# Gate and up products of the second token group by seven block products in place of eight

## What is computed

```
def _swiglu(x, w_gate, w_up, w_down):
    return (jax.nn.silu(x @ w_gate) * (x @ w_up)) @ w_down
...
x = _layer_norm(ALPHA * x + 0.5 * _swiglu(x, p['ffn1_gate'], p['ffn1_up'], p['ffn1_down']), p['ln1_g'], p['ln1_b'])
... projection, short convolution and sparse attention ("mix"), then attention into 256 memory tokens
x = _layer_norm(ALPHA * x + 0.5 * _swiglu(x, p['ffn2_gate'], p['ffn2_up'], p['ffn2_down']), p['ln4_g'], p['ln4_b'])
```

## Time and profile before

| | |
|---|---|
| time, median of 3 runs | 2527.73 us (2526.59 to 2529.33) |
| span of the profiled execution, first to last instruction | 2523.5 us |
| TensorE matmuls busy | 2437.7 us, 97% of the span, 16311 matmuls |
| VectorE, ScalarE, GpSimd busy | 36%, 39%, 55% |
| DMA | 245 MB, 97 GB/s in the mean, the 16 engines 33% busy |
| share of TensorE in the chain that ended last | 85% |

### The profile page before, as it was taken

The page is one execution under the profiler, slowest core; times in us unless marked ns, Lnnn a source line. Parts: engine busy times, 40 slices in busy tenths (PEclk is TensorE's granted clock), DMA queues, the critical chain, the costliest instruction groups (busy, mean ns, idle before and its releaser), DMA issues.

```text
span 2523.5 us, 39960 instructions
## 1 busy us (share of the span) xinstructions
PE 2437.7 (97%) x16311; PEld 2217.3 (88%) x16311; DVE 920.9 (36%) x1775; ACT 982.3 (39%) x1736; POOL 1376.1 (55%) x860
## 2 busy tenths in 40 slices
PE   8999999999999999998999999999899999999998
PEld 8888889888999999987789877888659899999998
DVE  1000002266810004277452689997264333000003
ACT  4333333534333233455543533333473435333231
POOL 4776665534666666422252676766405246666663
PEclk9999999999999999999999999999999999999999
DMA  4444532453233222533121234333402122433322
GB/s 145 123 119 117 159 94 75 139 156 104 83 94 91 86 84 79 141 107 125 45 76 35 70 102 106 110 92 100 166 1 88 48 68 81 121 109 101 92 84 69
DMA packets 425661, 245.00 MB, mean 97 GB/s; under 512 B 23008, under 2 KB 415328, under 8 KB 424720
## 3 DMA queue, kind: packets, MB, share of 16 engines
q1 hardware_dynamic: 389712, 197.88, 27.4%
q10 hardware_dynamic: 33200, 32.56, 4.0%
q0 software_dynamic: 2576, 12.07, 1.3%
HBM read 218.79 MB, written 21.74 MB: 95 GB/s over the span
## 4 chain that ended last, share of the span: by engine, by line
PE 85%; ACT 4%; DVE 4%; POOL 3%; issue 2%; DMA 1%; ACTq 0%; DVEq 0%; POOLq 0%
PE LIN L768 77%; PE TR L1109 1%; POOL WL L2093 1%; PE LIN L845 1%; PE TR L821 1%; ACT WH L1159 1%; POOL XL L2133 1%; ACT PR L1608 1%; ACT PT L1633 1%; PE LIN L1057 1%; PE TR L922 1%; DVE SC L1714 1%; PE TR L1096 1%; DVE PR L2032 1%; DVE CB L1958 1%
## 5 line engine op out<-in xcount | busy, mean ns | idle before, releaser
L2093 POOL TENSOR_TENSOR WL<-WRAW,WH 128x1024 fp32r<-128x1024 f32 (+1 forms) x378 | 889.3, 2355 | 473.9 <-ACT WH L1159 467.5
L768 PE MATMUL LIN<-XH,WH 128*128 128x256 f32 (+3 forms) x3032 | 838.2, 317 | 20.7 <-DVE Y L1782 6.5
L768 PE MATMUL LIN<-XH,WL 128*128 128x256 f32 (+3 forms) x3032 | 830.9, 315 | 0.0
L768 PE MATMUL LIN<-XL,WH 128*128 128x256 f32 (+3 forms) x3032 | 829.3, 314 | 0.0
L768 PEld LDWEIGHTS LIN<-XH,WH 128*128 128x128 f32 (+1 forms) x3032 | 529.0, 188 | 61.0 <-issue 20.0
L768 PEld LDWEIGHTS LIN<-XL,WH 128*128 128x128 f32 (+1 forms) x3032 | 528.8, 188 | 34.0
L768 PEld LDWEIGHTS LIN<-XH,WL 128*128 128x128 f32 (+1 forms) x3032 | 526.6, 188 | 33.8
L768 PE MATMUL LIN<-HH,WH 128*128 128x256 f32 (+2 forms) x1632 | 464.6, 307 | 1.7 <-POOL HL L2174 1.7
L768 PE MATMUL LIN<-HL,WH 128*128 128x256 f32 (+2 forms) x1632 | 462.1, 305 | 0.0
L768 PE MATMUL LIN<-HH,WL 128*128 128x256 f32 (+2 forms) x1632 | 461.4, 305 | 0.0
L1163 ACT ACTIVATE FG<-LIN 128x512 f32<-128x512 f32 (+3 forms) x270 | 154.9, 575 | 740.0 <-PE LIN L768 731.9
(11 more groups left out here) (200 smaller groups left out, 2048.2 us busy)
## 6 DMA issues: line engine op xcount, KB each, us to landing
WRAW<-in_ffn_gate SPq DMA_DIRECT2D x88, 512.0 KB, 3.8
WRAW<-in_ffn_up SPq DMA_DIRECT2D x88, 512.0 KB, 3.8
WRAW<-in_ffn_down SPq DMA_DIRECT2D x64, 512.0 KB, 3.8
WRAW<-in_w_mix_in SPq DMA_DIRECT2D x44, 512.0 KB, 3.8
WRAW<-in_ffn_down SPq DMA_DIRECT2D x32, 384.0 KB, 3.3
WRAW<-in_w_mix_out SPq DMA_DIRECT2D x16, 512.0 KB, 3.9
WRAW<-in_w_mem_q SPq DMA_DIRECT2D x16, 512.0 KB, 3.9
WRAW<-in_w_mem_o SPq DMA_DIRECT2D x16, 512.0 KB, 3.8
```

Source lines behind the costliest of these rows:

```text
L768: last = pe.matmul(LIN[0:pr.rows, pr.slot, out:out + w], wt[:, pr.tile % RING, c, 0:pr.rows], x[:, c, col:col + w], start=(c == 0 and wt i ...
L2093: pool.tensor_tensor(WL[:, n % RING, 0:nk, 0:width], WRAW[:, n % 2, 0:nk, 0:width], WH[:, n % RING, 0:nk, 0:width].bitcast(F32), ALU.subtr ...
```

## The change

It applies to group 1 only, in both feed-forwards. The gate and up matrices are seen as 2 x 2 blocks of 512 x 1408 (a, b left, top and bottom; c, d right), the tokens as 2 x 2 blocks of 512 features x 272 tokens. The tile u of the left half and the tile u + 11 of the right half form a unit. For units 1 to 9 of 11 the eight block products of a unit's gate (or up) are replaced by seven (the scheme of Strassen and Winograd), each of 4 chunks of weights and 272 tokens; units 0 and 10 stay as they were.

- *Weight sums* a+c, c+d, a+c+d and a+b+c+d of the four matrices are made in DRAM by 128 transfers on GpSimd's queue, 64 while group 0 is in the first feed-forward and 64 from its mixout on, one behind each product; half of them copy, half accumulate. Each moves 128 rows of 1408 floats (0.72 MB). A transfer waits for the one four products earlier.
- *Token sums*: four blocks of 128 x 1088 on VectorE, rounded on ScalarE, low parts on VectorE, within the first products of each feed-forward of group 1.
- *Mixing*: ScalarE copies two of the seven results (272 columns), VectorE combines the others in five instructions. The gate's Silu is taken in SBUF. Four banks of PSUM are used in turn.
- *Splits*: tiles of 4 chunks, eight places in the ring, six raw places; those of the seven products have their low part made on VectorE, the others on GpSimd.
- *Parts*: the hidden features are walked in five parts of 1, 2, 2, 2 and 4 units (2, 4, 4, 4 and 8 chunks for the down products) in place of three. The downs of the first part are added by VectorE, together with the factor ALPHA.
- *The selection of group 0* goes in single rounds behind down products (3 behind those of part 0, 7 behind each of the parts 1 to 3) and the last 8 behind unit 10's products.
- The memory keys and values make room for buffers: they are written to DRAM (two stores of 1 MB, waited for with the others of `memory turn`) and read back later.

```
+UNIT_PARTS = [[0], [1, 2], [3, 4], [5, 6], [7, 8, 9, 10]]
+WHOLE_UNITS = (0, PAIRS - 1)
+SEVEN = [("raw", 0, 0), ("sum", "acd", 0), ("sum", "cd", 0), ("sum", "ac", 0), ("raw", 4, 0), ("raw", 4, 1),
+         ("sum", "abcd", 0)]
+SUM_STEPS = [("ac", "a", False), ("cd", "c", False), ("ac", "c", True), ("cd", "d", True),
+             ("acd", "ac", False), ("acd", "d", True), ("abcd", "acd", False), ("abcd", "b", True)]
...
# the planner
+                for kind in ("gate", "up"):
+                    made += self.seven(which, g, kind, u, q, part)
...
+            turns = [(pr, 1) for pr in downs[0:KD:3]]
+            turns += [(pr, 1) for part in range(1, len(UNIT_PARTS) - 1) for pr in downs[KD * part:KD * part + 7]]
+            for k, pr in enumerate((ffn + mix)[2 * RING:][:2 * SUM_COUNT]):
+                pr.end.append(("weight sums", k))
...
+            for k, pr in enumerate((mixout + memq + memo + ffn)[:2 * SUM_COUNT]):
+                pr.end.append(("weight sums", 2 * SUM_COUNT + k))
...
# TensorE, product i of seven of matrix m
+            def one_of_seven(pr):
+                if i == 0 and before.name != "seven":
+                    for k in (before, PLAN.products[pr.p - 2]):
+                        pe.wait_ge(product_read[k.slot], k.turn + 1)
+                    pe.wait_ge(tok_lo, 4 * pr.which)
...
+                if i == 3:
+                    pe.wait_ge(seven_mixed, 5 * m + 1)
+                if i == 4:
+                    pe.wait_ge(seven_copied, 2 * m + 1)
+                if i == 5:
+                    pe.wait_ge(seven_mixed, 5 * m + 2)
+                if i == 6:
+                    pe.wait_ge(seven_mixed, 5 * m + 3)
...
+                for c in range(4):
+                    for wt, x in ((WH, 0), (WH, 1), (WL, 0)):
+                        last = pe.matmul(seven_bank(m, i), ring_place(wt, w)[:, c, :], moving(x, c), ...
...
# ScalarE; split_hi of the tiles that this product frees follows behind
+                if pr.j == 0:
+                    act.activation(SA[:, :], seven_bank(m, 0), ACT.Copy, scale=half).then_inc(seven_copied, 1)
+                    if pr.kind == "up":
+                        act.activation(GU[:, 0, NS:], GU[:, 0, NS:], ACT.Silu).then_inc(gated, 1)
...
+                if pr.j == 6 and pr.kind == "up":
+                    for k, side in enumerate((1, 0)):
+                        act.wait_ge(multiplied, pr.event + k + 1)
+                        act.activation(HH[:, pr.f + side, :], GU[:, 2 + side, :], ACT.Copy).then_inc(hidden_hi, 1)
...
# VectorE; split_lo of the tiles that this product frees follows behind and waits for hi_split
+                if pr.j == 1:
+                    dve.scalar_tensor_tensor(SU[:, :], seven_bank(m, 1), -half, SA[:, :], ALU.mult, ALU.add)
+                if pr.j == 3:
+                    dve.scalar_tensor_tensor(SV[:, :], seven_bank(m, 3), -half, SA[:, :], ALU.mult, ALU.add)
+                    dve.scalar_tensor_tensor(right[:, NS:GC], seven_bank(m, 2), -half, SV[:, :], ALU.mult, ALU.subtract)
+                if pr.j == 5:
+                    dve.scalar_tensor_tensor(right[:, 0:NS], seven_bank(m, 5), half, SA[:, :], ALU.mult, ALU.subtract)
+                if pr.j == 6:
+                    dve.scalar_tensor_tensor(left[:, NS:GC], seven_bank(m, 6), half, SU[:, :], ALU.mult, ALU.add)
...
# GpSimd
+                if pr.kind != "up" or pr.j != 6:
+                    return
+                for k, side in enumerate((1, 0)):
+                    pool.wait_ge(seven_mixed, 5 * m + 4 + k)
+                    pool.tensor_tensor(u, GU[:, side, :], u, ALU.mult).then_inc(multiplied, 1)
+                for k, side in enumerate((1, 0)):
+                    pool.wait_ge(hidden_hi, pr.event + k + 1)
+                    pool.tensor_tensor(HL[:, pr.f + side, :], u, HH[:, pr.f + side, :].bitcast(F32), ALU.subtract)
...
+            def weight_sums(k):
+                if made:
+                    pool.wait_ge(sums_made[r], 16 * made)
+                if adds:
+                    pool.dma_start(dst, src, accum_op=ALU.add).then_inc(sums_made[r], 16)
+                else:
+                    pool.dma_start(dst, src).then_inc(sums_made[r], 16)
```

More of the change, by code:

```diff
@@ L190, in stage @@
                     pr.tell(**facts, **more)
+                    if pr.kind == "down" and half is None and not pr.rescales:
+                        self.adds += 1
+                        pr.add = self.adds
                     made.append(pr)
@@ new lines, in seven @@
+    def seven(self, which, g, kind, u, q, part):
+        made = []
+        events = self.events
+        for i, (source, row, side) in enumerate(SEVEN):
+            if source == "sum":
+                w = self.weigh(("sum", which, kind, row), P * u, P, 0, 4, "dve", 6)
+            else:
+                w = self.weigh(f"ffn{which}_{kind}", P * (u + PAIRS * side), P, row, 4, "dve", 6)
+            pr = self.add(w.n, "seven", i, g, None, 4)
+            pr.tell(which=which, kind=kind, f=2 * q, part=part)
+            pr.matrix = self.sevens
+            pr.event = events
+            made.append(pr)
+        self.sevens += 1
+        if kind == "up":
+            self.events += 2
+            for half in (None, 0, 1):
+                self.hidden_done[which, g.index, part, 2 * q + 1, half] = events + 1
+                self.hidden_done[which, g.index, part, 2 * q, half] = events + 2
+        return made
@@ L340, in back @@
         else:
+            token_strands(ffn)
             ffn[2 * RING].mid.append(("gains",))
+            downs = [pr for pr in ffn if pr.kind == "down" and pr.half is None]
             for t in range(4):
-                ffn[12 + 12 * t].end.append(("early", t))
+                downs[KD + 1 + 6 * t].end.append(("early", t))
             last = [pr for pr in ffn if pr.half == 0][-4:]
@@ L371 @@
 NT = len(PLAN.weights)
+SEVENS_FIRST = 1 + max(pr.matrix for pr in PLAN.products if pr.name == "seven" and pr.which == 1)
+SEVEN_LAST_WEIGHTS = [PLAN.weights[pr.tile] for pr in PLAN.products if pr.name == "seven" and pr.which == 1][-1]
 MEMORY_UNITS = [(0, 0), (1, 0), (0, 1), (1, 1)]
@@ L388 @@
 TOK_AT = {0: 0, 1: len(GROUPS[0].tiles)}
-ADDED_AT = {(1, 0): 0, (1, 1): 2 * KD, (2, 0): 4 * KD, (2, 1): 7 * KD}
+ADDED_BEFORE_LAST = max(pr.add for pr in PLAN.products if pr.which == 2 and not pr.g.sample)
 EARLY = len(GROUPS[0].tiles)
@@ L1923, in take_up @@
                     select(GROUPS[what[0]])
+                elif kind == "select some":
+                    select_some(pairs_of(GROUPS[0])[0], what[0])
+                elif kind == "selection":
+                    selection(pairs_of(GROUPS[0])[0])
+                elif kind == "token sum":
+                    token_sum(*what)
+                elif kind == "token low":
+                    token_low(*what)
                 elif kind == "early":
@@ L2139, in take_up @@
                     norm_step(*what)
+                elif kind == "weight sums":
+                    weight_sums(*what)
                 elif kind == "early":
@@ L2239, in _ @@
                             for pr in prs:
[L2240 to L2241 removed]
+                                for n in PLAN.weights[pr.tile].frees if not ends and pr.last else ():
+                                    if PLAN.weights[n].low == "pool":
+                                        split_lo(n)
                                 for strand in pr.end if ends else ():
```

436 lines of the change are left out of this document (364 added, 72 removed).

## The result

The changed kernel takes **2709.7 us** (median of 4 runs, 2701.2 to 2718.5) against 2528.5 us beside it (4 runs, 2526.6 to 2529.9): a ratio of 1.0721, 95% interval 1.0696 to 1.0745. It is slower, as forecast, but by 181 us in place of 36, and outside the range. The profiled execution has a span of 2706.6 us, 183.1 more than before.

The account below looks back on a forecast made before the run. TensorE, busy 97% of the span, bounds the kernel. Matmuls saved -53.9, waits +80, waits lost today -2, weight sums +12 give +36 us: 2564 us; 8 in 10 range 2515 to 2640 us.

Parts of the forecast that it names:

- That weights come later does little: Group 0, weight tiles landing later beside the sum transfers: TensorE hardly waits; 8 us put down.
- The prices: Transfer engines' time per weight sum: 1.86 us for a copy, 3.7 us for an accumulating transfer, mean 2.8 us.
- The sum of demand: Group 0's first feed-forward: four sums and four tiles ask for 18.5 us of four products' 18.7 us; just fits.
- the sums overfill the transfer engines: Rival, chance 0.20: group 0's transfers exceed the time, GpSimd stands waiting; 2629 us, or 2750 us with dearer copies.
- What goes: Group 1's gate and up products, both feed-forwards: 432 matmuls fewer, 53.9 us saved.
- Within a unit: Between a unit's seven short products in group 1: VectorE and ScalarE keep up, costed at nothing.
- Unit after unit: Where one unit of seven follows another, product 3 waits 2.6 us, ten times: 26 us (12 to 32).
- The selection behind the later downs: Selection rounds behind later down products delay the next unit's product 3, plus PSUM changes: 11 us (2 to 14).
- The ends of the parts: Ends of parts 1 to 3, both feed-forwards: down products wait 4.2 us six times, 25 us (19 to 27).
- Part 0: First part's eight short downs in each feed-forward: VectorE falls behind, 15 us (10 to 20).
- the waits stay short: Rival, chance 0.22: every group 1 wait at its lower bound, 44 us, sums cost 4; 2520 us.
- nearly cancel: Rival, chance 0.08: whole kernel, savings and costs nearly cancel; 2523 to 2533 us.

Follow-up runs that it names:

- e1: The changed kernel without its 128 weight-sum transfers, the seven products loading raw matrix blocks of the same size instead: 2598.9 us, ratio 1.0279.
- e2: The kernel before with the 128 weight-sum transfers added at the same places, their results unused: 2638.5 us, ratio 1.0440.
- e11: The changed kernel with all sum transfers issued at an eighth of their columns, the seven products loading unsummed weights: 2604.1 us, ratio 1.0298.
- e7: The changed kernel with the low parts of weight tiles in group 0's first feed-forward made by VectorE in place of GpSimd: 2742.3 us, ratio 1.0853.
- e3: The changed kernel with every accumulating transfer made a plain copy of the same rows: 2652.6 us, ratio 1.0483.
- e4: The changed kernel with the same 128 sum transfers spread over all products of group 0's two stretches: 2676.5 us, ratio 1.0593.

## Why the prediction was wrong

**The failed step** is "That weights come later does little: a tile that landed after 12.38 us left TensorE busy in the ten microseconds beside it ... I put 8 us". These 8 us measured 111 (e1) and 110 (e2); the 4 us beside them, for the stores, agree with the 3.7 us by which group 0's first read-out is late in e1. The prices were right: 1.83 and 3.6 us of the transfer engines against my 1.86 and 3.7. The sum of demand was right too, 18.5 us of 18.7: 83% of 350 us are 290 us of the transfer engines' time, all of the 290 us that the stretch had taken before. From "it fits" I concluded "it does not wait". But nothing was to spare: in the longer stretch the engines are still at 90% or more in 15 of the 35 windows of 10 us from 50 to 400 us (before: in none), and TensorE is idle beside full transfer engines, as in the second of these rows (the view's shares of short windows are rough and can pass 1):

```profile
172.00:176.00 4.00, 4.00 (x19) 3.24 (x18) 0.00 (x0) 0.00 (x0) 0.43 (x1) 1.00 1.07 211
176.00:180.00 4.00, 0.79 (x4) 0.31 (x2) 0.00 (x0) 0.00 (x0) 0.00 (x0) 0.91 1.04 218
```

And a load cannot run far ahead, since two raw buffers are all there is. A tile is consumed every 4.67 us (14.0 us for three), so a turn may take 9.3 us; rounding and low part take 1.05 and 2.4 of it, and some 5.8 us are left for the landing. It took 3.8 us before. In the changed kernel the medians from 60 to 460 us are:

```profile
WRAW<-in_ffn_up SPq DMA_DIRECT2D x18, 512.0 KB, 5.9
WRAW<-in_ffn_gate SPq DMA_DIRECT2D x17, 512.0 KB, 6.6
...
WRAW<-in_w_mem_k SPq DMA_DIRECT2D x6, 512.0 KB, 7.8
```

and 4.0, 4.0 and 4.1 in e11. The late tile of the earlier trace rows was a single one, with up to four finished tiles in the ring, and my window ended at 1530 us, ahead of its landing at 1533.3; TensorE was idle for 0.43 of the six microseconds from 1530 on. A row of such tiles empties the ring. This reading fits e1 and e11. It failed on e7, where landings grew as the turn got shorter, and the medians alone do not order the versions either (6.1 us for the gates in e3, and 57 us less). The other reading, that the engines are full in bursts, orders e11, e3, e4 and the changed kernel (none, 3, 6 and 15 windows at 90% or more; 5, 54, 78 and 111 us), but not e7 (12 windows, 33 us more). How the bytes become waits, by full engines or by landings through two buffers, therefore stays open; that the bytes and the adding make the cost is shown.

**The rival "the sums overfill the transfer engines"** gave 2629 and 2750 us, nearer than the forecast, by another way. Its stall, GpSimd standing before a sum, is 8.7 us in all, 8.0 of them in 3 waits, where it had 73 or 195 us; what it says of full engines is not refuted (above). The Trainium skill (DMA: Bandwidth & Descriptors, Latency and other measured facts), with 207 to 214 GB/s for copies between HBM tensors, led to "near 2700 us". The measured time lies there by luck: a copy took 1.83 us of the engines, 394 GB/s, where that rate gives 3.4 us as an estimate, and with 3.4 us for a copy and 5.6 for an adding one the prediction's own working gives 2732 us.

**The second omission** is the clock. 0.96 over both changed stretches is 34 us, more than any of the five terms of waiting, and over the whole kernel it is some 73 us by the estimate above. The windows around one part end in the second feed-forward show how it arises:

```profile
2500.00:2509.00 9.00, 9.00 (x74) 9.00 (x73) 1.71 (x5) 4.67 (x9) 6.89 (x6) 1.00 0.61 170
2509.00:2516.00 7.00, 3.19 (x24) 2.78 (x22) 0.87 (x2) 2.46 (x4) 7.00 (x6) 1.00 0.63 182
2516.00:2523.00 7.00, 6.73 (x41) 6.73 (x42) 1.42 (x1) 1.45 (x3) 2.85 (x3) 0.76 0.20 58
2523.00:2530.00 7.00, 7.00 (x59) 7.00 (x58) 3.03 (x3) 3.12 (x6) 3.35 (x3) 1.00 0.25 72
```

TensorE is idle for 3.8 of 7 us at full clock (3.39 of them before a down product, for `HL`), and then works for a while at 0.76 on average, part of the time at its lower level of 1.2 GHz: 7 x 0.24 = 1.7 us more, after the wait is over. From 709 us on, with 3.3 us of idle in the first, two windows in a row show 0.70 and 0.81.

**The terms of group 1, by the prediction's steps.** *What goes*: 15879 matmuls, right. 192 of the new ones ran in 24.37 us in the chain, 126.9 ns each for 124.7. *Within a unit*: costed at nothing, right; no such wait is among the rows. *Unit after unit*: 26 us forecast; ten of the eleven waits for `SU` are these, each of 2.5 us, five in each feed-forward at the places foreseen, 24.8 us together, and for the stated reason. VectorE, ScalarE and GpSimd at one such boundary, in the order of time:

```profile
2319.09 1.37 POOL L2612 TENSOR_TENSOR GU<-GU 128x544 f32<-128x544 f32 x1 [33.35 <-DVE GU L2360]
2319.24 1.76 DVE L2003 TENSOR_TENSOR WL<-WRAW,WH 128x512 fp32r<-128x512 f32 x1 [0.23 <-ACT WH L1415]
...
2322.83 0.66 ACT L1761 ACTIVATE HH<-GU 128x544 fp32r<-128x544 f32 x1 [1.68 <-POOL GU L2612]
2323.39 0.61 ACT L1415 ACTIVATE WH<-WRAW 128x512 fp32r<-128x512 f32 x1
2323.91 0.38 ACT L1744 ACTIVATE SA<-LIN 128x272 f32<-128x272 f32 x1
2324.04 2.44 DVE L2003 TENSOR_TENSOR WL<-WRAW,WH 128x512 fp32r<-128x512 f32 x2 [2.69 <-ACT WH L1415]
...
2326.40 0.43 DVE L2347 SCALAR_TENSOR_TENSOR SU<-LIN,SA 128x272 f32<-128x272 f32 x1
```

The subtraction started 0.15 us behind GpSimd's multiplication takes 1.76 us in place of 0.69, and the second multiplication, `HH`, `SA`, `SU` follow in the forecast order. It ended 0.54 us after GpSimd's instruction (2321.00 and 2320.46 us), which agrees with the lock that the Trainium skill states (SBUF — State Buffer, Who interferes with whom). Over the run VectorE's 512-wide splits have a mean of 0.86 us. *The selection behind the later downs*: 9 us forecast in the first feed-forward, where the rows have no such wait of product 3, and 2 in the second, where the eleventh wait stands, 4.5 us up to 2386.9 us: VectorE had group 0's outputs to normalise behind the downs, which my walk left out. *The ends of the parts*: 25 forecast, 20.4 measured in 6. *Part 0*: the downs wait 4.9 and 6.9 us for `HL` and 2.3 and 1.3 us for `Y`, and 3.3 us stand in front of the first unit of the first feed-forward with no releaser shown. GpSimd has four and six splits of down tiles ahead of its multiplication there (a piece "7.33 POOL WL L2501 x6" in the chain at 2273.76), of which my walk had one or two; so the 15 us are a right size with a partly wrong content. All waits together 83 us for 78.

**The rival "the waits stay short"** (2520 us) is refuted by the same rows; "nearly cancel" as well. Of my tests ahead of the run, the one that spoke was the last: "if group 0's stretches grow by over 20 us"; they grew by 119.

## What to carry to other kernels

Saved matmuls are paid out only if the shorter products still cover the chains between the other engines; cost every change of unit and part as a wait, and add what the clock takes after it. For traffic that is put beside weight loads, a demand that just fits (18.5 us of 18.7) is not free: ask how much of the stretch the transfer engines keep to spare, and compare the landing time that the buffers allow (turns x product time, less the steps that free a buffer) with what landings become. Which of the two decides was not separated here. A quick way to know is to add the transfers, unused, to the old kernel: e2 gave the 110 us without any of the rest.

## What the runs showed of the hardware

An accumulating transfer from DRAM to DRAM of 704 KB took about twice the engines' time of a copy (3.6 for 1.83 us) and cost more than in proportion: 57 of 111 us for the 64 of 128 transfers that add. The engines' time is no fixed price: the same 45.42 MB took 42.7% of 400 us in the changed kernel and 47.2% in e7. What a wait of TensorE does to the clock is not the same each time. The wait of 2.47 us that ended at 2326.97 us left it at 1.00 (first two rows); one as long, ended at 819.90 us, was followed by 0.76 (last two):

```profile
2320.00:2327.00 7.00, 4.53 (x37) 4.34 (x36) 4.20 (x6) 3.68 (x7) 4.96 (x4) 1.00 0.36 105
2327.00:2334.00 7.00, 7.00 (x56) 7.00 (x57) 4.69 (x9) 3.37 (x6) 0.00 (x0) 1.00 0.40 111
814.00:821.00 7.00, 4.53 (x37) 4.34 (x36) 4.16 (x6) 3.09 (x7) 4.50 (x3) 1.00 0.33 95
821.00:828.00 7.00, 7.00 (x46) 7.00 (x45) 3.50 (x7) 2.95 (x6) 0.00 (x0) 0.76 0.26 76
```

Making an engine step shorter (e7) lengthened the landings of most of the loads that it released, from 5.9 to 11.1 us for one of the matrices, and shortened those of the gates from 6.6 to 4.4 us; it stays open why.
